# A gate projected features by tokens from split parts and applied behind the output's turning, and modulation products moved into two solver levels

## The reference

```python
mod = jax.nn.silu(c) @ w_mod[l] + b_mod[l]
sh1, sc1, gt1, sh2, sc2, gt2 = jnp.split(mod[:, None, :], N_MOD, axis=-1)
h = rms_norm(x, g_mix[l]) * (1.0 + sc1) + sh1
dn_qkv, dn_z, dn_b, dn_a, c_q, c_kv, k_r, gates = jnp.split(h @ w_in[l], split_at, axis=-1)
qkv = silu(centred_depthwise_conv(dn_qkv, conv_w))          # 8 heads of 128 features
...                                                          # per head, both directions:
t_inv = triangular_solve(eye + lower, eye)                   # chunks of 64 tokens
u, w = t_inv @ v_beta, t_inv @ (k_beta * exp(gc))
v_new = u_i - w_i @ state
o_i = qd_i @ state + intra_i @ v_new
...
o = rms_norm(o_fwd + o_bwd, o_gain) * jax.nn.silu(z)         # z: dn_z of the head
```

## Time and profile before

| what | value |
|---|---|
| median of 3 runs | 2677.28 us (2676.2 to 2678.05) |
| profiled execution: time / span | 2677.34 us / 2675.4 us |
| TensorE busy | 2610.0 us, 98% |
| VectorE / ScalarE / GpSimd busy | 38% / 32% / 30% |
| granted TensorE clock, mean | 0.996 |

### The profile page before, as it was taken

One profiled execution on the slowest core, in us unless ns is written; L12 is line 12 of the kernel. 1 busy time (PEld: TensorE's weight loads), 2 busy tenths in 40 slices (PEclk: granted clock), 3 DMA queues, 4 the chain that ended last, 5 costly groups with the idle time before them and its releaser, 6 DMA issues.

```text
span 2675.4 us, 35978 instructions
## 1 busy us (share of the span) xinstructions
PE 2610.0 (98%) x14664; PEld 1999.3 (75%) x14664; DVE 1026.1 (38%) x1880; ACT 850.0 (32%) x1483; POOL 806.7 (30%) x643
## 2 busy tenths in 40 slices
PE   7999999999999999999998899999999999999998
PEld 4888888885568885444543897988888987988887
DVE  4676677524322152221222796300011785200012
ACT  3544444423332241000001437322223246322222
POOL 2232333300124320000000442344455433344453
PEclk9999999999999999999999999999999999999999
DMA  7122211311114248999999221332222321232221
GB/s 245 40 76 95 79 63 39 110 61 46 52 37 130 91 167 372 426 426 427 426 426 408 95 80 33 95 95 95 95 95 81 103 70 50 86 102 95 95 95 47
DMA packets 189624, 384.53 MB, mean 144 GB/s; under 512 B 11953, under 2 KB 146997, under 8 KB 163893
## 3 DMA queue, kind: packets, MB, share of 16 engines
q1 hardware_dynamic: 188288, 381.69, 38.4%
q10 hardware_dynamic: 1205, 0.99, 0.1%
HBM read 380.55 MB, written 2.10 MB: 143 GB/s over the span
## 4 chain that ended last, share of the span: by engine, by line
PE 86%; DVE 5%; ACT 3%; DVEq 2%; DMA 1%; issue 1%; SPq 1%; ACTq 0%; POOL 0%
PE bank L1765 14%; PE bank L1770 14%; PE bank L1769 14%; PE bank L2055 12%; PE bank L2002 2%; PE bank L1560 2%; PE bank L1631 1%; PE bank L1622 1%; PE bank L1526 1%; PE bank L1524 1%; PE bank L1525 1%; PE bank L1819 1%; DVE conf L3030 1%; PE bank L1541 1%; PE bank L1836 1%
## 5 line engine op out<-in xcount | busy, mean ns | idle before, releaser
L767 POOL TENSOR_TENSOR w_lo<-ring,w_hi 128x512 fp32r<-128x512 f32 x384 | 522.6, 1393 | 666.8 <-ACT w_hi L817 666.8
L817 ACT ACTIVATE w_hi<-ring 128x2048 fp32r<-128x2048 f32 x96 | 184.0, 1917 | 619.5 <-PE bank L1765 619.5
L1765 PE MATMUL bank<-hT_hi,w_hi 128*128 128x512 f32 (+1 forms) x944 | 356.7, 378 | 8.3 <-DVE hT_lo L2960 6.2
L1770 PE MATMUL bank<-hT_hi,w_lo 128*128 128x512 f32 (+1 forms) x944 | 351.6, 372 | 0.0
L1769 PE MATMUL bank<-hT_lo,w_hi 128*128 128x512 f32 (+1 forms) x944 | 351.3, 372 | 0.0
L1765 PEld LDWEIGHTS bank<-hT_hi,w_hi 128*128 128x128 f32 x944 | 179.0, 190 | 39.9 <-issue 6.1
L1770 PEld LDWEIGHTS bank<-hT_hi,w_lo 128*128 128x128 f32 x944 | 178.8, 189 | 31.0
L1769 PEld LDWEIGHTS bank<-hT_lo,w_hi 128*128 128x128 f32 x944 | 179.0, 190 | 30.1 <-issue 1.0
L3171 DVE TENSOR_TENSOR ffn_hT<-ffn_sg,bank 128x512 f32<-128x512 f32 x44 | 30.2, 687 | 414.8 <-PE bank L1770 414.8
L738 POOL TENSOR_TENSOR solve_S<-l_neg,level_mask 128x512 f32<-128x512 f32 x56 | 80.4, 1442 | 360.3 <-DVE l_neg L2572 343.8
L767 POOL TENSOR_TENSOR w_lo_m<-ring,w_hi_m 128x512 fp32r<-128x512 f32 x64 | 82.4, 1319 | 302.1 <-ACT w_hi_m L817 302.1
(11 more groups left out here) (551 smaller groups left out, 5346.6 us busy)
## 6 DMA issues: line engine op xcount, KB each, us to landing
ring<-in_w_gate SPq DMA_DIRECT2D x56, 1024.0 KB, 7.5
ring<-in_w_down SPq DMA_DIRECT2D x52, 1024.0 KB, 7.0
ring<-in_w_up SPq DMA_DIRECT2D x46, 1024.0 KB, 8.7
place<-in_w_up SPq DMA_DIRECT2D x40, 1024.0 KB, 18.2
place<-in_w_down SPq DMA_DIRECT2D x34, 1024.0 KB, 25.0
ring<-in_w_in SPq DMA_DIRECT2D x33, 1024.0 KB, 5.2
place<-in_w_gate SPq DMA_DIRECT2D x30, 1024.0 KB, 23.9
head_w<-in_w_in SPq DMA_DIRECT2D x32, 512.0 KB, 7.4
```

Of the source, the lines that this page charges most:

```text
L767: last = pool.tensor_tensor(w_lo[m % 2][:, cs], src[:, cs], w_hi[m % 2][:, cs].bitcast(F32), ALU.subtract)
L817: return act.activation(dst, src, ACT.Copy)
L1765: first = mm(dst, a[0], b[0], start=start, stop=False)
L1770: return mm(dst, a[1], b[0], start=False, stop=stop)
```

## The change

Gate: `project_z` now multiplies split parts, `wz_hi` and `wz_lo` by `hd_hi` and `hd_lo`, features by tokens, in 24 matmuls of 512 columns. `wz_hi` lies where `decay` lies and is made by ScalarE behind level five; `wz_lo` is written over the raw weights by VectorE behind the solver, together with the first two weight remainders that were made at the turn's end. The gate is applied after the turning: VectorE multiplies bank 5 by the gain and `z_silu` into `oT_dn` (`gated`) and counts `head_done`; ScalarE's scaling goes. Modulation: the eight products go to levels four and five, four each. On TensorE the decay rows move ahead of the values' turning.

```diff
+        wz_hi = at("wz_hi", XN_AT, [P, KD, HD], F32R)
+        wz_lo = at("wz_lo", HEADW_AT, [P, KD, 512], F32R)[:, :, 3 * HD:4 * HD]
@@ SyncE
             load_mod2(HEADS - 1)
+            sp.wait_ge(sem("z_done"), HEADS)
@@ ScalarE, opening
             act.wait_ge(sem("qkv_w_then_place_11_in"), 48 + 32)
             high_part(1).then_inc(step["w_hi_first_1"], 1)
+            def high_z():
+                return copy(wz_hi[:], head_w[:, :, 3 * HD:4 * HD])
+            act.wait_ge(sem("z_w_then_place_12_in"), 16)
+            high_z().then_inc(step["z_hi_first"], 1)
             reached(act, "gc_ready")
...
-            act.sem_inc(sem("head_done"), 1)
@@ ScalarE, head
+                    if lv == 5:
+                        if more:
+                            act.wait_ge(sem("z_w_then_place_12_in"), h * 16 + 32)
+                            act.wait_ge(sem("intra_masked"), h * 2 + 2)
+                            high_z().then_inc(once_a_turn["z_hi_ready"], 1)
...
-                    in_turn(act, "o_ready", h)
+                    act.wait_ge(sem("head_done"), h + 2)
                     take_z(h + 1)
...
-                in_turn(act, "oT_done", h)
-                act.activation(oT_dn[...], bank[5][:], ACT.Copy,
-                               scale=cols_a[:, R_OG:R_OG + 1]).then_inc(sem("head_done"), 1)
@@ TensorE
             def project_z(h):
-                pe.wait_ge(sem("z_w_then_place_12_in"), h * 16 + 16)
-                for t in range(TT):
-                    for k in range(KD):
-                        last = mm(bank[2][:, t * P:(t + 1) * P], hT[:, k, t * P:(t + 1) * P], head_w[:, k, 3 * HD:4 * HD],
-                                  start=k == 0, stop=k == KD - 1)
+                if isinstance(h, int) and h == 0:
+                    reached(pe, "z_lo_first")
+                else:
+                    in_turn(pe, "z_lo_ready", h - 1)
+                for k in range(KD):
+                    mm(bank[2][:], wz_hi[:, k, :], hd_hi[:, k, :], start=k == 0, stop=False)
+                    mm(bank[2][:], wz_hi[:, k, :], hd_lo[k][:], start=False, stop=False)
+                    last = mm(bank[2][:], wz_lo[:, k, :], hd_hi[:, k, :], start=False, stop=k == KD - 1)
...
+                def modulation(half):
+                    if half == 0:
+                        pe.wait_ge(sem("raw_ready"), h * 3 + 5)
+                        pe.wait_ge(sem("mod2_w_then_place_13_in"), h * 16 + 16)
+                    for g in range(4):
+                        k = half * 4 + g
+                        last = mm(bank[0][g * 32:g * 32 + 32, :], silu_cb[:, k, :], mod2_w[:, k, :], start=half == 0, stop=half == 1)
+                        if half == 1:
+                            last.then_inc(sem("mod2_done"), 1)
...
+                    if lv in (4, 5):
+                        modulation(lv - 4)
                     pe.wait_ge(sem("N_ready"), h * 6 + lv)
...
-                for k in range(KD):
-                    g = k % 4
-                    last = mm(bank[0][g * 32:g * 32 + 32, :], silu_cb[:, k, :], mod2_w[:, k, :], start=k < 4, stop=k >= 4)
@@ VectorE, opening
             dve.drain().then_inc(step["g_ready"], 1)
+            def low_z():
+                return tt(wz_lo, head_w[:, :, 3 * HD:4 * HD], wz_hi[:].bitcast(F32), ALU.subtract)
+            reached(dve, "z_hi_first")
+            low_z().then_inc(step["z_lo_first"], 1)
             conv(0, 1)
@@ VectorE, head
+                in_turn(dve, "z_hi_ready", h)
+                if split:
+                    low_part(0)
+                    low_part(1)
+                if more:
+                    low_z().then_inc(once_a_turn["z_lo_ready"], 1)
...
                 dve.wait_ge(sem("u_ready"), h * 2 + 2)
...
-                in_turn(dve, "z_ready", h)
                 for t in range(TT):
-                    stt(o_tok[:, t, :], bank[7][:, t * P:(t + 1) * P], o_scale[:, t:t + 1], z_silu[:, t, :], ALU.mult, ALU.mult)
+                    ts(o_tok[:, t, :], bank[7][:, t * P:(t + 1) * P], o_scale[:, t:t + 1], None, ALU.mult)
                 dve.drain().then_inc(once_a_turn["o_ready"], 1)
+                def gated():
+                    in_turn(dve, "z_ready", h)
+                    in_turn(dve, "oT_done", h)
...
+                    stt(dst, bank[5][:], cols_a[:, R_OG:R_OG + 1], z_silu[:], ALU.mult, ALU.mult).then_inc(sem("head_done"), 1)
                 if more:
                     head_columns(h + 1)
+                    gated()
                     if split:
                         in_turn(dve, "w_hi_ready", h + 1)
-                        for part in range(3):
-                            last = low_part(part)
-                        last.then_inc(once_a_turn["w_lo_ready"], 1)
+                        low_part(2).then_inc(once_a_turn["w_lo_ready"], 1)
```

More of the change, by code:

```diff
@@ L151, in build @@
         q_sq = at("q_sq", r.pos - 4096, [P, SEQ])
-        z_silu = r("z_silu", [P, TT, P])
+        z_silu = r("z_silu", [P, SEQ])
         knT = r("knT", [P, SEQ])
@@ L380, in build @@
             "vector_steps": (
-                "eps_ready", "cols_ready", "silu_cb_ready", "mod1_part_1", "mod1_part_3", *(f"mod1_taken_{j}" for j in range(4)), "mod1_cols", "h_lo_ready", "sp_in", "g_ready", "angles_ready", "gc_ready", "mod2_copied",
+                "eps_ready", "cols_ready", "silu_cb_ready", "mod1_part_1", "mod1_part_3", *(f"mod1_taken_{j}" for j in range(4)), "mod1_cols", "h_lo_ready", "sp_in", "g_ready", "z_lo_first", "angles_ready", "gc_ready", "mod2_copied",
                 "latent_diag_0", "gate1_copied", "latent_diag_1", "gate2_copied", "kr_ready", "mod2_ready", "shift_summed",
@@ L411, in build @@
             "head_vector": (
-                "head_q_ready", "w_lo_ready", "k_tok_ready", "intra_ready", "o_ready",
+                "head_q_ready", "w_lo_ready", "k_tok_ready", "intra_ready", "z_lo_ready", "o_ready",
             ),
@@ L417, in build @@
             "head_scalar": (
-                "w_hi_ready", "z_ready", "v_tok_ready", "o_rms",
+                "w_hi_ready", "z_ready", "v_tok_ready", "z_hi_ready", "o_rms",
             ),
@@ L935, in take_z @@
                 act.wait_ge(sem("z_done"), h + 1)
-                act.activation(flat_rows(z_silu[:]), bank[2][:], ACT.Silu).then_inc(once_a_turn["z_ready"], 1)
+                act.activation(z_silu[:], bank[2][:], ACT.Silu).then_inc(once_a_turn["z_ready"], 1)
             def key_squares(h):
@@ L983, in head @@
                         next_high(lv - 3)
+                    if lv == 5:
[4 more added lines that the diff above has]
+                        else:
+                            act.drain().then_inc(once_a_turn["z_hi_ready"], 1)
                 for d in range(2):
@@ L1015, in head @@
                     keep_ckv(0)
-                in_turn(act, "oT_done", h)
-                act.activation(oT_dn[:, h:h + 1, :].rearrange("p a n -> p (a n)") if isinstance(h, int) else oT_dn[:, bass.ds(h, 1), :].rearrange("p a n -> p (a n)"), bank[5][:], ACT.Copy,
-                               scale=cols_a[:, R_OG:R_OG + 1]).then_inc(sem("head_done"), 1)
+                    act.drain().then_inc(step["ckv_kept"], 1)
             reached(act, "angles_ready")
@@ L1099, in _ @@
                             reached(act, "mod2_turned")
+                            act.wait_ge(sem("head_done"), 1 + HEADS)
                         src_hi(o_dn_hi, oT_dn, (n,))
@@ L1593, in head @@
                     last.then_inc(sem("gc_row_done"), 1)
+                pe.wait_ge(sem("head_done"), h + 1)
+                to_tokens(h, 2, 5)
                 fill(0, 0, KD)
@@ L1682, in head @@
                     latent_q(3)
-                pe.wait_ge(sem("raw_ready"), h * 3 + 5)
-                pe.wait_ge(sem("mod2_w_then_place_13_in"), h * 16 + 16)
-                for k in range(KD):
-                    g = k % 4
-                    last = mm(bank[0][g * 32:g * 32 + 32, :], silu_cb[:, k, :], mod2_w[:, k, :], start=k < 4, stop=k >= 4)
-                    if k >= 4:
-                        last.then_inc(sem("mod2_done"), 1)
                 if not more:
@@ L1720, in _ @@
             for b in range(4):
+                if b == 3:
+                    reached(pe, "ckv_kept")
                 turn_latent(b)
@@ L2538, in _ @@
             tt(col_q[:, 2], col_q[:, 2], col_q[:, 0], ALU.mult)
-            dve.drain()
+            dve.drain().then_inc(sem("head_done"), 1)
             def head_columns(h):
@@ L2594, in head @@
                        tri[:, d:d + 1, :].to_broadcast([P, TT, P]), ALU.mult).then_inc(sem("TT_ready"), 1)
+                in_turn(dve, "z_hi_ready", h)
[4 more added lines that the diff above has]
+                    low_z().then_inc(once_a_turn["z_lo_ready"], 1)
+                else:
+                    dve.drain().then_inc(once_a_turn["z_lo_ready"], 1)
                 dve.wait_ge(sem("u_ready"), h * 2 + 2)
```

6 lines of the change are left out of this document (3 added, 3 removed).

## The result

| kernel | median, us | lowest to highest | runs | ratio to before | 95% interval |
|---|---|---|---|---|---|
| before | 2677.28 | 2675.91 to 2678.98 | 13 | | |
| changed | 2684.71 | 2678.28 to 2686.11 | 13 | 1.0023 | 1.0015 to 1.003 |

The change makes the kernel 7.4 us slower by the medians; forecast were 2676.2 and a range that ended at 2681.8. The runs of the changed kernel spread more than those of the kernel before: most lie between 2684.4 and 2686.1 at a mean granted clock of 0.992 or 0.993, three between 2678.3 and 2678.8 at 0.995, one at 2681.4. These four are why the ratio in the table is smaller than that of the medians (1.0028): the means are only 5.8 us apart. The profile is of a run of the longer kind: span 2683.0, time 2684.86, clock 0.992, against 2675.4, 2677.34 and 0.996.

A forecast was written before the change was run, and what follows sets the result against it. TensorE was taken to bound the kernel, except the opening, bound by a VectorE and ScalarE chain. Heads −8.1, opening +6.5 and clock +0.5 sum to −1.1: 2676.2 us from 2677.28, range 2671.0 to 2681.8.

The forecast's parts named there:

- What bounds: Opening before head 0: a chain through VectorE's convolution and ScalarE, not TensorE; at a head's end: TensorE, without gaps.
- Opening, 6.5 us lost: Before head 0, VectorE waits for ScalarE's gate split, so the convolution starts at 64.8, not 58.30: 6.5 us lost once.
- End of a head, 2.64 won: Gate projection to next projection: the next starts at 257.35, not 259.99, behind the third remainder; 2.64 us won in six heads.
- Modulation in the levels, 0.8 each: Solver levels four and five: four products each, 0.16 us hidden, 0.8 us lost a level, 1.6 a head.
- Head 6: End of head 6, where no remainder is made: 3.5 us won, against 1.6 lost in its levels.
- head 7: Head 7: the modulation's 1.86 us comes in whole in the levels and goes out whole at the end: zero.
- The clock, +0.5 (bounds 0 to 2.5): Opening, after TensorE stands 6.8 us until 78.0: work at half clock costs 0.5 us beyond the keys' slack.
- Slower: VectorE's middle slot overflows: VectorE's wait before the states: three remainders, 3.6 us, overfill its 5.34 us and delay each head; 2685, chance 0.06.
- Slower: the opening's clock: TensorE at half speed from 78 until well into head 0 costs 5.6 us, not 0.5: 2681.3; chance 0.06.
- The levels and the tail give little: Levels cost 1.0 each, bank product 0.99, more waiting at the output: 5.5 us worse, 2681.7; chance 0.04 within the band.

The follow-up runs named there:

- the run with that edit alone: Kernel before, with only head 0's gate weights split in the opening and its projection taking them: 2683.93 us, ratio 1.0028.
- the edit with the levels alone: Kernel before, with only the modulation products moved into levels four and five from behind the output's turning: 2685.53 us, ratio 1.0037.
- the second: Profile from repeating the changed kernel with no edit, taken of its fastest run, 2678.62 us; median 2684.1 us, ratio 1.0022 against the kernel before.

## Why the prediction was wrong

- **What bounds.** Right in both parts: the opening by VectorE's convolution, a head's end by TensorE.
- **Opening, 6.5 us lost.** Right: 6.37 in the profile, and 6.28 from the landing of the load in both the change and the run with that edit alone. The 6.8 by which that run is slower hold some clock as well.
- **End of a head, 2.64 won.** Right: 2.56 in a looped head, with the third remainder as the last wait, as forecast. VectorE's middle slot did not overflow; its wait before the states is still 1.96.
- **Modulation in the levels, 0.8 each.** Mis-sized: 0.93 to 0.94. I let the 0.16 between the fill and the product count as a wait that the products could fill; they filled 0.07 of it, and their block takes 1.00, not 0.93 and the 0.03 for setting up. In a head that is 1.88 against 1.6. Head 6 gave 1.5 (period 61.46 against 62.96), not 1.9, and head 7 cost 0.1. With them the heads won 5.8 against 8.1; the edit with the levels alone shows that this part of the change is a loss in the kernel before too.
- **The clock, +0.5 (bounds 0 to 2.5).** This is the step that failed. For the opening it was in its bounds: 1.7 in the first profile, 0.9 in the second. But the term ended there: it priced the clock only behind the wait that the change makes, and had nothing for work that the change only shifts. In the profiled run 3.2 us were lost near 600 under lines that the change doesn't touch; laying the one-column products apart takes 3.3 off the changed kernel's median and 1, not told from none, off that of the kernel before. Another 2.1 came in behind 700, part of them clock and 1.5 a wait for VectorE near 1580, for which the sum had no term either. The mis-sized levels (2.3) and the opening's clock (1.2 over the 0.5) would by themselves have left the time at 2679.7 (an estimate from these differences), inside the range; the stretch near 600 took it out. With both places near 78 and 600 at full clock, the change measures 2678.6, within the range.
- **The rivals.** "Slower: VectorE's middle slot overflows" has the number that lies nearest, 2685, and nothing of its cause: the wait that it needs gone is still 1.96. "Slower: the opening's clock" (2681.3) had the right engine and the wrong place: in the opening the clock cost 1.7, not 5.6. "The levels and the tail give little" was right in direction, with 2.3 of its 5.5.
- What stays open: why the clock falls at the one-column products in some runs and not in others, what makes TensorE wait 1.77 or 0.29 for VectorE near 1580, and how the medians (of which each kernel's profile shows one run) divide over these places.

## What to carry to other kernels

The wait that the change put into VectorE's in-order queue cost what was queued behind it, whole, even though the waiting work (1.2 us) is small: it could be placed where that engine stands anyway (which here still cost 1.5, as TensorE then waited), or avoided by giving the one odd case the old form. Work moved "under a wait" has to be compared with the wait in its old place and the new one; here the new place hid almost none of it, and the old one half in the changed kernel (0.90 of 1.85 showed) and three quarters in the kernel before (0.46 of 1.86). And where a change shifts thin stretches of TensorE's work, put the clock into the range, at each such stretch, in kernels with an effect of a few tenths of a per cent, and take a second profile before a difference of some us is put down to a place.

## What the runs showed that I had not expected

- TensorE's granted clock fell to 0.50 with no idle gap in its work, among 32 one-column instructions, and that took 3.2 us (those 32 in 4.46 instead of 3.82, the next 32, of 128 columns, in 6.39 instead of 3.82).
- The same kernel had this in one profiled run and not in another; their spans differ by 6.2 us, 4.5 of it by the end of that work.
- The clock was low at this work in seven of ten profiles with the one-column instructions in a row, and in none of four with them laid apart.
- 5.4 us of idle turnings took 5 us off a kernel's median (3.7 off its mean). The clock stayed at 1.00 while they ran; by the landmarks of the opening that accounts for 0.5 to 1.5 of it.
- A 32-column block between 128-column ones in a solver's level takes 1.00 for eight instructions; behind the turning sixteen take 1.85.
